# Merge pass of a gated attention and SSD layer: gates opened and scaled two turns ahead, weight loads one unit ahead

## The reference

```python
proj = rms_norm(x, norm_gain) @ w_in            # q | k | v | z_attn | z_ssd | xBC | dt | gate_logits
branch_a = (window_attention(q, k, v, ...) * silu(z_a)) @ w_attn_proj
y_s = rms_norm(ssd_mixer(xbc, dt, ...) * silu(z_s), ssd_norm_gain)
branch_b = y_s @ w_ssd_proj                     # 2048 -> 1024 channels
g_a, g_b = split(sigmoid(gate_pre + b_gate))    # 1024 channels each
merged = g_a * branch_a + g_b * branch_b
x = x + merged @ w_out
```

## Time and profile before

| | |
|---|---|
| median of 3 runs | 1498.97 us (1498.94 to 1499.01) |
| the profiled execution | 1494.86 us |
| its span | 1493.0 us |
| PE busy | 1441.3 us, 97% |
| DVE busy | 721.3 us, 48% |
| ACT busy | 542.1 us, 36% |
| POOL busy | 461.9 us, 31% |
| mean DMA rate | 142 GB/s |

### The profile page before, as it was taken

How to read it: one execution, slowest core, us unless ns; L and a number is a source line. 1 busy time by engine, 2 the same in 40 slices (tenths; PEclk the granted TensorE clock), 3 DMA queues, 4 the chain that set the end, 5 groups by cost and what they waited for, 6 DMA issues and landing times.

```text
span 1493.0 us, 21406 instructions
## 1 busy us (share of the span) xinstructions
PE 1441.3 (97%) x7424; PEld 1151.1 (77%) x7424; DVE 721.3 (48%) x794; ACT 542.1 (36%) x998; POOL 461.9 (31%) x230
## 2 busy tenths in 40 slices
PE   5999999999999997999999999999999999999999
PEld 4878888888888886777777777777777888787787
DVE  5369764444444004454545555454566454465411
ACT  6242223323323114352535354342536643422200
POOL 1221221221221122332233332332235665534321
PEclk9999999999999999999999999999999999999999
DMA  5212212222222246676585869686666536534321
GB/s 211 71 50 99 88 67 107 89 85 107 89 86 106 90 152 133 190 143 198 151 193 157 228 151 181 192 151 196 138 239 244 196 136 201 198 114 168 128 97 72
DMA packets 164665, 212.43 MB, mean 142 GB/s; under 512 B 6320, under 2 KB 127408, under 8 KB 164640
## 3 DMA queue, kind: packets, MB, share of 16 engines
q1 hardware_dynamic: 127888, 163.60, 39.0%
q10 hardware_dynamic: 36656, 48.37, 9.0%
q0 software_dynamic: 96, 0.13, 0.0%
HBM read 150.87 MB, written 61.21 MB: 142 GB/s over the span
## 4 chain that ended last, share of the span: by engine, by line
PE 49%; issue 39%; POOL 6%; DVE 2%; ACT 2%; DMA 1%; POOLq 0%; ACTq 0%; DVEq 0%; SPq 0%
PE F L152 32%; POOL sb_whl L162 4%; PE F L1347 3%; PE M L1347 3%; PE M L667 2%; PE M L710 2%; DMA sb_acc<-cs_d 1%; POOL sb_res L1171 1%; ACT sb_early L912 1%; PE F L704 1%; PE F L697 1%; PE F L681 1%; PE M L660 1%; PE M L704 1%; PE M L697 1%
## 5 line engine op out<-in xcount | busy, mean ns | idle before, releaser
L152 PE MATMUL F<-sb_X,sb_whl 128*128 128x512 f32 x4800 | 1153.2, 400 | 7.2 <-DVE sb_X L392 2.9
L152 PEld LDWEIGHTS F<-sb_X,sb_whl 128*128 128x128 f32 x4800 | 903.3, 189 | 236.5 <-issue 17.0
L162 POOL TENSOR_TENSOR sb_whl<-sb_wst,sb_whl 128x1024 fp32r<-128x1024 f32 x109 | 272.9, 2503 | 870.4 <-ACT sb_whl L159 870.0
L159 ACT ACTIVATE sb_whl<-sb_wst 128x1024 fp32r<-128x1024 f32 x109 | 115.4, 1059 | 247.1 <-PE F L152 120.3
L938 ACT ACTIVATE sb_res<-F 128x512 f32<-128x512 f32 x64 | 38.5, 601 | 199.1 <-PE F L152 193.1
L480 DVE SCALAR_TENSOR_TENSOR sb_early<-F,sb_acc,sb_early 128x1023 f32<-128x1023 f32 (+2 forms) x72 | 92.3, 1281 | 10.5 <-DVE sb_early L478 0.2
L478 DVE TENSOR_SCALAR sb_early<-F,sb_acc 128x1024 f32<-128x1024 f32 x24 | 30.8, 1284 | 134.6 <-PE F L152 134.6
L442 DVE TENSOR_TENSOR sb_early<-sb_early 32x1024 f32<-32x1024 f32 x40 | 65.4, 1636 | 31.8 <-ACT sb_early L340 31.2
L833 DVE TENSOR_TENSOR sb_early<-sb_early 128x1024 f32<-128x1024 f32 x32 | 50.1, 1585 | 63.5 <-ACT sb_early L929 63.5
L929 ACT ACTIVATE sb_early<-sb_acc,sb_ncs_sb 128x128 f32<-128x128 f32 x256 | 77.4, 393 | 6.6 <-PE M L697 6.6
L1235 DVE SCALAR_TENSOR_TENSOR sb_X<-sb_X,sb_cst x16 | 54.6, 3412 | 35.8 <-POOL sb_part L1158 35.8
(11 more groups left out here) (154 smaller groups left out, 1196.8 us busy)
## 6 DMA issues: line engine op xcount, KB each, us to landing
sb_wst<-w_units SPq DMA_DIRECT2D x109, 512.0 KB, 3.7
sb_acc<-cs_d SPq DMA_DIRECT2D x8, 2048.0 KB, 20.5
x_d<-sb_res ACTq DMA_DIRECT2D x24, 512.0 KB, 2.7
z_d<-sb_res ACTq DMA_DIRECT2D x24, 512.0 KB, 2.7
sb_early<-x_d SPq DMA_DIRECT2D x8, 1024.0 KB, 7.8
sb_acc<-ecs_d SPq DMA_DIRECT2D x16, 512.0 KB, 24.1
g_d<-sb_res ACTq DMA_DIRECT2D x16, 512.0 KB, 4.4
y_d<-sb_acc ACTq DMA_DIRECT2D x8, 1024.0 KB, 17.6
```

What stands on the lines that cost most here:

```text
L152: last = nc.tensor.matmul(bank, whl[:, slot, wp, k, :], act[:, ap, k, half * HALF:(half + 1) * HALF], start=(k == 0 and wp == 0 and ap == ...
L159: return nc.scalar.activation(whl[:, slot, 0], wst[:, slot], ACT.Copy)
L162: return nc.gpsimd.tensor_tensor(whl[:, slot, 1], wst[:, slot], whl[:, slot, 0].bitcast(f32), ALU.subtract)
```

## The change

Three edits, all in the merge pass:

1. ACT and POOL: the loops are written out. The gates of turns 0 and 1 are opened (`gate_open`) and scaled (`gate_norm`) before turn 0, and turn m then opens and scales the gate of turn m+2. On ACT this stands at the end of turn m, after its second `merged_high`; on POOL after the `low` of unit 18+m.
2. SP: the weights of units 18 and 19 are loaded ahead of the first `load_merge`, and ahead of the wait for the norm's sum (`sq_done`) before it.
3. SP: turn m loads the weights of unit 20+m, where before it loaded those of unit 18+m; the load now stands behind the turn's wait for `m_lo` and its `load_merge`, and ahead of `load_rows`. The separate loads of units 24 and 25 fall away, since the turns now cover them.

```diff
+            for s in range(2):
+                load_w(sp, B3 + 18 + s, 0, 0)
             sp.wait_ge(sq_done, 16)
             for s in range(2):
                 load_merge(0, s)
...
             with nc.sync.Fori(0, 3) as i:
                 for s in range(2):
-                    load_w(sp, B3 + 18 + s, 2, i)
                     sp.wait_ge(m_lo, i * 4 + (2 * s + 2))
                     load_merge(i + 1, s)
+                    load_w(sp, B3 + 20 + s, 2, i)
                     load_rows(i, s)
-            for s in range(2):
-                load_w(sp, B3 + 24 + s, 0, 0)
...
             pool.wait_ge(rms_ready, 1)
-            with nc.gpsimd.Fori(0, 4) as i:
-                for s in range(2):
-                    pool.wait_ge(gateB_ready, i * 2 + (s + 1))
-                    nc.gpsimd.tensor_tensor(gate[:, s, :], gate[:, s, :], ms, ALU.mult).then_inc(gr_ready, 1)
-                    low(pool, B3 + 18 + s, 2, i)
+            def gate_norm(n):
+                pool.wait_ge(gateB_ready, n + 1)
+                nc.gpsimd.tensor_tensor(gate[:, n % 2, :], gate[:, n % 2, :], ms, ALU.mult).then_inc(gr_ready, 1)
+
+            gate_norm(0)
+            gate_norm(1)
+            for n in range(8):
+                low(pool, B3 + 18 + n, 0, 0)
+                if n + 2 < 8:
+                    gate_norm(n + 2)
...
-            with nc.scalar.Fori(0, 4) as i:
-                for s in range(2):
-                    act.wait_ge(merge_in[s], i * 32 + 32)
-                    nc.scalar.activation(gate[:, s, :], gate[:, s, :], ACT.Sigmoid,
-                                         bias=C("b_gate", 8, 16)[:, ds(i * 2 + s, 1)]).then_inc(gateB_ready, 1)
-                    merged_high(i, s, 0)
-                    high(act, B3 + 18 + s, 2, i)
-                    merged_high(i, s, 1)
+            def gate_open(n):
+                act.wait_ge(merge_in[n % 2], (n // 2) * 32 + 32)
+                nc.scalar.activation(gate[:, n % 2, :], gate[:, n % 2, :], ACT.Sigmoid,
+                                     bias=C("b_gate", 8, 16)[:, n:n + 1]).then_inc(gateB_ready, 1)
+
+            gate_open(0)
+            gate_open(1)
+            for n in range(8):
+                merged_high(n // 2, n % 2, 0)
+                high(act, B3 + 18 + n, 0, 0)
+                merged_high(n // 2, n % 2, 1)
+                if n + 2 < 8:
+                    gate_open(n + 2)
```

More of the change, by code:

```diff
@@ L1209, in merged_high @@
                 to = slice(h * HALF, (h + 1) * HALF)
-                nc.scalar.activation(split_tile(X0, 0, i, s)[:, to], acc_tile(i, s)[:, to], ACT.Copy).then_inc(m_hi, 1)
-            with nc.scalar.Fori(0, 4) as i:
-                for s in range(2):
-                    act.wait_ge(merge_in[s], i * 32 + 32)
-                    nc.scalar.activation(gate[:, s, :], gate[:, s, :], ACT.Sigmoid,
-                                         bias=C("b_gate", 8, 16)[:, ds(i * 2 + s, 1)]).then_inc(gateB_ready, 1)
-                    merged_high(i, s, 0)
-                    high(act, B3 + 18 + s, 2, i)
-                    merged_high(i, s, 1)
+                nc.scalar.activation(X0[:, 0, 2 * i + s, to], acc[:, 2 * i + s, to], ACT.Copy).then_inc(m_hi, 1)
+            def gate_open(n):
[10 more added lines that the diff above has]
+                    gate_open(n + 2)
             with nc.scalar.Fori(0, 3) as i:
```

## The result

The changed kernel takes 1508.03 us (median of 4, 1506.81 to 1509.86), the kernel before in the same comparison 1498.99 us (1498.94 to 1500.84): ratio 1.0059, 95% interval 1.0046 to 1.0072. That is slower by 9.0 us, where 11.6 were forecast; the forecast time was 1510.6 us. Its profiled execution took 1506.81 us, its span is 1505.0 us.

The account below looks back on a forecast made before the run. A ring through the other engines, 12.7 us a turn, was taken to pace TensorE's 11.2; the new ring's 14.55 over six turns, with start, end and clock, added 11.6 us: 1510.6 us, range 1503.5 to 1518.5.

Parts of the forecast that it names:

- The new ring: Merge pass: gate transfer, sigmoid, merged_high, GpSimd and VectorE up to the next m_lo, 14.55 us a turn against 12.7 before.
- D(m): End of merge turn m's last VectorE subtraction, which is m_lo; D(0) forecast at 1325.0, D(6) at 1412.3.
- two blocks by GpSimd: Each turn, VectorE's first-half subtraction and second-half multiply wait for GpSimd's scaling and low part; about 3.1 us together.
- written-out code, under 0.3 us in all: ScalarE's and GpSimd's merge turns written out instead of looped: either way under 0.3 us in all.
- The start: Before turn 0: later gate transfers and the second gate's scaling put D(0) at 1325.0 instead of 1322.8.
- TensorE: Merge pass: stops of 3.3 us ahead of units 20 to 24; last stage's first group into F 11.4 us later.
- The clock: A lower TensorE clock after stops makes a unit 13.2 us, still under the ring's 14.55; could cost up to 2 us.
- The rival in which the clock stays low: Units 20 to 23 and some of 24 take 22.4 us instead of 11.2: 35 us on top, 1546; 2%.
- The range: Whole kernel: likeliest case from about 1504 to 1519 us; stated forecast range 1503.5 to 1518.5.
- The sign that the sigmoid starts no earlier than 4 us after m_lo: ScalarE, each turn: a sigmoid starting less than 4 us after the previous turn's m_lo would show the forecast wrong.
- the case "no change": Time within 0.2% (3 us), ring between 12.2 and 13.2 us, needing one block and about 0.5 us to vanish; 5%.
- the order wins: Rival: merge ring at most 11.2 us, TensorE's 8.7 us of stops go, 1490.3 us; 4%, some partial win 3% more.

Follow-up runs that it names:

- the first experiment: The kernel before with the two SyncE edits alone, ScalarE's and GpSimd's loops and gate order unchanged: 1497.56 us, ratio 1.0002.
- the two good orders: Changed kernel with gates opened one turn ahead, 1489.71 us; changed kernel with gates opened behind the next turn's split and GpSimd's low part before scaling, 1489.78 us.

## Why the prediction was right

**The new ring** was right as a mechanism, step by step: transfer issued after D(m), sigmoid waiting for it ahead of ready work, two blocks by GpSimd, in that order. Three experiments each shortened or lengthened a different piece of it (transfer, scaling, GpSimd's order), and the turns came out at 13.0, 13.1 and 15.0 us where 12.9, 12.95 and 15.0 had been worked out. The control that moves nothing but the sigmoid's place takes the turns from 15.0 to 11.3 us.

**Its length** was sized a little high: 14.55 forecast, 14.23 measured, 1.9 us over six turns. About half of the 0.32 is the transfer: in the turn above the sigmoid starts 5.06 after m_lo, and I had it at 5.2. About 0.1 is the second merged_high, which follows its sum by 0.03 us (VectorE's row at 1382.34, length 0.69, then ScalarE's at 1383.06), where in loop form the gap is 0.14 (1358.94 + 0.69 to 1359.77 in the first experiment) and I had counted 0.15. The rest are small offsets in my chain. So "written-out code, under 0.3 us in all" was mis-sized: this gap alone gets shorter in each turn, over 0.6 us in six.

**The start** was right: D(0) forecast 23.3 us after unit 16's start, measured 22.98. The second gate's scaling blocks the first multiply, where I had it block the addition behind it; the end is the same. I had spaced the landings of the five transfers unevenly, by 0.8 to 1.3 us, though I had read 1.3 for each; that didn't show in D(0).

**TensorE**: the last stage was to start 107.9 us after unit 16, it started 105.80 after it; the first group into F 115.3, and it was 113.04. All of the difference is the ring's length and the start. The stops ahead of the units 19 to 23 and the last stage were 0.47, 2.82, 1.27, 2.96, 2.54 and 2.91 us, where I had forecast 3.3 ahead of each of units 20 to 24: the shorter ring takes about 0.3 of each, and the stop of 1.27 is shorter by another 1.5 because the unit ahead of it ran slow.

**The clock**: the earlier trace rows let me price a drop after such a stop; it came after some. The changed kernel, stretches as in the earlier trace rows (granted clock is the third number from the end):

```profile
1351.00:1365.00 14.00, 11.61 (x43) 9.30 (x44) 8.01 (x8) 3.25 (x4) 4.84 (x3) 0.88 0.41 150
1380.00:1394.00 14.00, 11.45 (x48) 8.92 (x48) 8.21 (x9) 3.25 (x4) 5.04 (x3) 1.00 0.41 150
1394.00:1409.00 15.00, 11.43 (x48) 8.92 (x48) 8.97 (x10) 3.25 (x4) 5.92 (x3) 1.00 0.38 140
1409.00:1425.00 16.00, 14.67 (x56) 11.65 (x57) 10.10 (x11) 2.84 (x4) 3.52 (x2) 0.89 0.21 71
```

The unit behind the stop of 2.82 us took 12.96, the group behind 2.91 took 7.40 instead of 5.86; behind 2.96 and 2.54 the clock stayed at 2.4 GHz. As forecast, it cost nearly nothing: TensorE was waiting for the ring anyway. The unit behind the first drop ended late by 1.5 us, and the next stop was 1.27 us instead of 2.8. The group of 7.40 us, the last of the merge stretch, cost next to nothing too: the group behind it started 4.66 us after D(6), where in three experiments with a group of 5.86 us there it started after 4.64. The Trainium skill ("TensorE: Matmul & The Clock Gate", section "Why this matters for your kernels") warns of long idle gaps between bursts of matmuls, since they give the lower clock back. Of the four stops of 2.5 to 3.0 us here two were followed by it, so at this length a stop's length alone doesn't tell. The rival in which the clock stays low did not happen.

**The range and the signs.** The upper end of the range was added up wrongly: 1510.6 + 8.7 + 1.5 is 1520.8 and not 1519. Nothing hangs on it, since the time came out below the forecast. As a sign I had named a wait of some 4 us ahead of each sigmoid; it was 5.8 to 6.0. I had counted from when the sum was ready, but ScalarE is idle from its last merged_high on, 0.85 us ahead of m_lo. The sign that the sigmoid starts no earlier than 4 us after m_lo held, at about 5.0. And the case "no change" needed less than I had said: I had it need one block and half a microsecond besides to vanish, while the experiment without the scaling lost that one block and came out with turns of 13.14 us, level with the kernel before.

**What I had not seen**, and what the first experiment's expectation got wrong: the ring of the turn's own work. It played no part in the forecast, since the new ring is longer. But "the order wins" needed it to be no longer than TensorE's 11.2 us too, and that it is only because edit 1 writes the loops out (12.0 us on the mean in loops, 11.06 written out). For that case I had forecast a gain of 8.7 us; the two good orders win 8.3 us of merge stretch, and 7.5 and 7.4 us by the medians (1489.71 and 1489.78 beside 1497.19).

## What to carry to other kernels

Work "ahead" must be placed behind everything that is ready before its input can be there: ask when the transfer is issued (here: when the buffer of two turns ago comes free), add its landing time, and put the wait at that point of the in-order list, not earlier. When a ring is cut, write down the next one with its length before promising the gain. Here there were three: 14.2 us in the changed kernel, under it 12.7 through the weights where SyncE's list is as before, and under that 12.0 of the turn's own work in loops. And an instruction that the compiler adds at a loop's head, like a table load, may be hidden until the ring over it is cut.

## What the runs showed of the hardware

- A VectorE instruction with both inputs in SBUF that starts while GpSimd works on SBUF ended 0.54 to 0.56 us after GpSimd's instruction, however early it started (2.36 and 2.00 us for 0.69 of work), and went between two GpSimd instructions that follow each other at once, the second of which then took 2.7 to 2.9 instead of 2.4. The additions from PSUM took 0.63 to 0.69 us in the merge pass of every profiled kernel, beside GpSimd or not. The Trainium skill ("SBUF — State Buffer", section "SBUF: two separate sides") calls it an exclusive lock held for the whole instruction, and names VectorE's instructions with two SBUF inputs; these rows agree.
- Stops of TensorE of 2.82 and 2.91 us were followed by a lower clock, stops of 2.54 and 2.96 us were not, in one and the same execution of the changed kernel.
- The sigmoid's table was loaded in every loop iteration although only copies stood between two sigmoids, 1.28 us each; written out, once.
